# Block inverse of a chunked RWKV recurrence: products over four array quadrants, both head groups as one, identity preset by GpSimd, masked copies

## The chip, the cores and the metric

One core of a Trainium2 chip runs the whole program. Its engines are TensorE (PE in the profile, its weight loads PEld), VectorE (DVE), ScalarE (ACT), GpSimd (POOL) and SyncE (SP). The metric is device microseconds of one execution; lower is better. All tensors named here are float32, and each float32 product of 64x64 blocks leaves two matmul records and two weight-load records in the trace.

## The reference, cut to what matters

The reference is one mixer-and-feed-forward block followed by a two-layer block with experts. The change touches one piece alone: the two RWKV recurrences of the second block's first layer (forward and reversed), over 8 heads of 64 and 768 tokens (256 context tokens, then 512).

```python
def wkv7_scan(state0, r, w, k, v, a_vec, b_vec, reverse):
    def step(S, inp):
        r_t, w_t, k_t, v_t, a_t, b_t = inp
        sa = jnp.einsum('bhij,bhj->bhi', S, a_t)
        S = (S * w_t[:, :, None, :] + sa[..., None] * b_t[:, :, None, :]
             + v_t[..., None] * k_t[:, :, None, :])
        return S, jnp.einsum('bhij,bhj->bhi', S, r_t)
    s_fin, ys = lax.scan(step, state0, xs, reverse=reverse)
```

The kernel doesn't walk token by token. It takes chunks of 64 tokens, and inside a chunk the feedback of `sa` on itself is a unit lower triangular 64x64 system for each head and direction, which it inverts.

## The kernel before, in words

The program is a list of stages, and each stage writes out by hand what TensorE, ScalarE, VectorE and GpSimd do, in order, with semaphores between them. An engine's queue is strictly in the written order, so a wait holds up all that is written behind it. The recurrence is the stage `Wkv` (lines 1960 to 2325), and no other stage runs beside it. It makes `STEPS` = 768/64 = 12 steps, one for each chunk.

In a step there are 16 blocks of 64x64: tile `c` (4), head `e` in the tile (2), direction `d` (2). The 16 blocks of one kind lie in 128 partitions x 512 columns. A product whose operands are read from partitions 64i and whose result is written to partitions 64j uses the array's quadrant (row half i, column half j).

A step n, in the order of the work:
1. ScalarE `exps` (lines 2169, 2170), GpSimd `keyed` and `more_factors` (2290 to 2304), and VectorE `new_keys` and `factors` (2207 to 2226) make the decayed operands `at`, `rt`, `bt`, `kt`; for step n+1 they run inside step n.
2. TensorE multiplies operands against each other, "grams" (`gram`, line 2044). Kinds 0 and 1 give the triangular matrix L and its transpose; kinds 2 to 4 give matrices for values and outputs. Line 2059 transposes `vc`, `bt`, `kt` (12 transposes of 128x128), which ScalarE copies out of PSUM (2176).
3. VectorE masks gram 0 to `lt` and gram 1 to `x`, masks `lt` to `xt`, and adds the identity to both (2231, 2238, 2240, 2241). `x` is the inverse so far and `xt` its transpose.
4. Five levels (`LEVELS`) double the size of the inverted blocks. In each, GpSimd masks the blocks that join (2319, `lo`), TensorE multiplies `lo` by `x` (`half`), ScalarE copies the result to `t1` (2181), TensorE multiplies `t1` by `xt` and `xt` by `t1` (`whole`), and VectorE adds the results to `x` and `xt` (2250, 2251).
5. The right side (`from_state` 2104 and 2108, `from_keys` 2115 and 2120) is copied (2187) and multiplied by the inverse (the last use of line 2071, giving `u`), copied (2191), and goes into the state's and the output's sums (2140, 2145, 2150). VectorE adds and decays the state (2265, 2268) and adds the output to `y` (2273).

Steps 3 and 4 run for two groups `g`: tiles 0 and 1, then tiles 2 and 3, each 256 columns wide. The products of the inverse all go through one helper, which reads partitions of direction d and writes partitions of direction d, so it uses two quadrants:

```python
def diagonal(out, lhs, rhs, g, start=True, stop=True):
    for c in (2 * g, 2 * g + 1):
        for e in (0, 1):
            for d in (0, 1):
                last = t.matmul(self.by_token(out, c - 2 * g, e, d), self.by_token(lhs, c, e, d), ...
```

At a step's start TensorE waits for `factors`, multiplies grams 0 and 1 of group 0, waits for `y_added` of the step before (the output sums share PSUM banks 0 and 1 with group 1's grams), and goes on.

## Time and profile before

| what | us |
|---|---|
| median of 3 runs | 3028.18 (3023.76 to 3029.92) |
| the profiled execution | 3029.54 |
| its span, first to last instruction | 3027.8 |
| the stage `Wkv` in it, 1388.2 to 1754.7 | 366.5 |
| one step in it that kept the full clock, 1573.04 to 1602.76 | 29.72 |
| PE busy over the span, share | 2583.5, 85% |
| DVE / ACT / POOL busy, share | 1751.9, 58% / 1192.6, 39% / 388.3, 13% |

The profiled execution takes 1.7 us more than its span, and 1.4 us more than the median. Times in the trace count from the span's start. PE busy counts a matmul from its start to its modelled end; matmuls overlap, so the share of busy time is not the share of the peak. The granted clock (PEclk) is 1.00 at 2.4 GHz and 0.50 at 1.2 GHz.

### The profile page before, as it was taken

Reading aid. Unit: us, or ns where it says so; the run is one execution under the profiler, and the core shown is the slowest. Engines: PE = TensorE matmul, PEld = TensorE weight load, DVE = VectorE, ACT = ScalarE, POOL = GpSimd, SP = SyncE. Lnnn points to the kernel's source line nnn. Section 1 sums busy time; section 2 is a strip of 40 time slices with the busy share of each in tenths; the row PEclk is TensorE's granted clock in tenths of the full one; section 3 lists DMA queues with packets and bytes.
Section 4 is the critical chain, followed back from the end, with each engine's and each line's share of the span. In section 5 each row is a group of like instructions: output and inputs, shape, how many; then the busy total and the mean of one; then the engine's idle time right before and its main releaser. Section 6 shows DMA issues by size and latency. Waiting matters only on the chain.

```text
span 3027.8 us, 55155 instructions
## 1 busy us (share of the span) xinstructions
PE 2583.5 (85%) x23020; PEld 1975.1 (65%) x23020; DVE 1751.9 (58%) x2676; ACT 1192.6 (39%) x1719; POOL 388.3 (13%) x447
## 2 busy tenths in 40 slices
PE   6979779999976899988888887889976889978995
PEld 5745457777764457855777755767765656756774
DVE  3655554445433654446777664579975265447985
ACT  2423432223132155233222223267754247435773
POOL 1010010000011110003343401111111030011211
PEclk9978989999998799987999988999997989989998
DMA  4257722222210000100000031189992200017996
GB/s 167 90 182 283 288 70 84 83 83 111 83 58 32 6 1 38 34 22 2 4 4 4 4 140 47 63 350 400 403 368 96 77 1 2 29 61 289 407 389 235
DMA packets 63817, 385.10 MB, mean 127 GB/s; under 512 B 7840, under 2 KB 7856, under 8 KB 27104
## 3 DMA queue, kind: packets, MB, share of 16 engines
q1 hardware_dynamic: 41792, 292.60, 25.2%
q0 software_dynamic: 21792, 89.16, 7.7%
q8 instruction: 175, 2.87, 0.4%
q14 instruction: 58, 0.48, 0.0%
HBM read 344.99 MB, written 36.70 MB: 126 GB/s over the span
## 4 chain that ended last, share of the span: by engine, by line
PE 68%; DVE 10%; issue 4%; DVEq 4%; ACT 4%; PEld 3%; DMA 2%; POOL 1%; PEldq 1%; ACTq 1%; POOLq 0%; SPq 0%
PE psum L396 15%; PE psum L598 12%; PE psum L2985 6%; PE psum L2071 4%; PE psum L1124 4%; PE psum L3006 3%; PE psum L1143 2%; PE psum L1134 2%; PE psum L1763 2%; PE psum L2633 2%; PE psum L378 2%; PEld psum L2985 2%; PE psum L1670 2%; DVEq L2252 1%; PE psum L982 1%
## 5 line engine op out<-in xcount | busy, mean ns | idle before, releaser
L396 PE MATMUL psum<-arena_r 128*128 128x512 f32 (+1 forms) x976 | 311.4, 360 | 9.0 <-issue 4.0
L598 PE MATMUL psum<-arena_r 128*128 128x512 f32 x704 | 250.3, 396 | 27.4 <-DVE weight_slots_r L683 13.8
L396 PE MATMUL psum<-arena_r,weight_slots_r 128*128 128x512 f32 (+1 forms) x696 | 247.9, 356 | 0.0
L416 ACT ACTIVATE arena_r<-weight_slots 128x1024 fp32r<-128x1024 f32 x73 | 76.4, 1057 | 341.1 <-PE psum L396 255.6
L396 PEld LDWEIGHTS psum<-arena_r 128*128 128x128 f32 x976 | 178.9, 190 | 46.6 <-issue 20.2
L598 PE MATMUL psum<-arena_r,weight_slots_r 128*128 128x512 f32 x528 | 207.2, 392 | 0.0
L2071 PE MATMUL psum<-x_t 64*64 64x64 f32 x5376 | 180.3, 220 | 30.7 <-DVEq L2252 15.2
L2071 PEld LDWEIGHTS psum<-x_t 64*64 64x64 f32 x5376 | 166.4, 135 | 42.6 <-DVEq L2252 20.1
L396 PE MATMUL psum<-h_t_r,arena_r 128*128 128x512 f32 (+1 forms) x528 | 191.1, 362 | 0.3
L2957 DVE TENSOR_TENSOR weight_slots_r<-weight_slots,arena_r 128x2048 fp32r<-128x2048 f32 x78 | 177.5, 2287 | 17.8 <-ACT arena_r L2952 17.5
L2957 DVE TENSOR_TENSOR weight_slots_r<-weight_slots,h_t_r 128x2048 fp32r<-128x2048 f32 x72 | 164.1, 2288 | 19.8 <-ACT h_t_r L2952 19.2
L598 PEld LDWEIGHTS psum<-arena_r 128*128 128x128 f32 x704 | 132.3, 190 | 63.8 <-issue 31.9
L1208 DVE TENSOR_REDUCE stat<-psum 128x1 f32<-128x768 f32 (+1 forms) x112 | 98.7, 882 | 108.9 <-PE psum L1124 108.8
L2985 PE MATMUL psum<-weight_slots_r,arena_r 128*128 128x512 f32 x400 | 158.4, 396 | 0.0
L2952 ACT ACTIVATE arena_r<-weight_slots 128x2048 fp32r<-128x2048 f32 x78 | 148.6, 1912 | 24.2 <-DMA weight_slots<-in_weights 24.0
L2952 ACT ACTIVATE h_t_r<-weight_slots 128x2048 fp32r<-128x2048 f32 x72 | 137.2, 1913 | 26.3 <-DMA weight_slots<-in_weights 26.2
L396 PEld LDWEIGHTS psum<-arena_r,weight_slots_r 128*128 128x128 f32 x696 | 132.0, 190 | 18.9
L2985 PE MATMUL psum<-arena_r 128*128 128x512 f32 x416 | 135.1, 407 | 10.7 <-issue 10.2
L598 PE MATMUL psum<-h_t_r,arena_r 128*128 128x512 f32 x352 | 138.0, 392 | 0.0
L1124 PE MATMUL psum<-arena 64*128 64x384 f32 (+2 forms) x416 | 121.9, 535 | 8.6 <-POOL arena L1174 4.9
L2985 PE MATMUL psum<-h_t_r,arena_r 128*128 128x512 f32 x384 | 120.7, 395 | 2.1 <-issue 1.8
L421 DVE TENSOR_TENSOR weight_slots_r<-weight_slots,arena_r 128x1024 fp32r<-128x1024 f32 x73 | 88.4, 1220 | 53.1 <-ACT arena_r L416 52.2
(455 smaller groups left out, 5442.6 us busy)
## 6 DMA issues: line engine op xcount, KB each, us to landing
weight_slots<-in_weights SPq DMA_DIRECT2D x277, 1024.0 KB, 7.3
y_rows<-arena POOLq DMA_DIRECT2D x50, 512.0 KB
h_rows<-arena POOLq DMA_DIRECT2D x10, 512.0 KB, 3.0
x_keep<-x_t POOLq DMA_DIRECT2D x1, 3072.0 KB, 9.0
x_t<-x_keep POOLq DMA_DIRECT2D x1, 3072.0 KB, 14.5
x_t<-in_x POOLq DMA_DIRECT2D x1, 2048.0 KB, 10.0
out_x<-x_t SPq DMA_DIRECT2D x1, 2048.0 KB, 7.2
arena<-in_toe POOLq DMA_DIRECT2D x1, 1792.0 KB, 8.6
```

The costliest lines, as they stand in the source:

```text
L378: last = self.nc.tensor.matmul(self.bank(n), w[:, kt, :], self.operand(part, kt, a, b), start=(kt == order[0] and i == 0), stop=(kt == ord ...
L396: last = self.nc.tensor.matmul(self.bank(n), w[:, kt, :], self.operand(part, kt, a, b), start=(i == 0), stop=(i == len(passes) - 1))
L416: self.nc.scalar.activation(self.w_hi[:, t % 2], self.tile_weights(self.kern.slots, t), ACT.Copy).then_inc(self.rounded[0], 1)
L421: self.nc.vector.tensor_tensor(out=self.tile_weights(self.kern.slots_r, t), in0=self.tile_weights(self.kern.slots, t), in1=self.w_hi[:, t ...
L598: last = nc.tensor.matmul(bank, w(p, k), x(q, k), start=(k == j == 0), stop=(k == n - 1 and j == 2))
L1124: last = t_.matmul(s[:, r, a:b], q, key[:, a:b], start=True, stop=True)
L1208: v.reduce_max(kern.row_max[:, par], self.score_bank(u), mybir.AxisListType.XY)
L2071: last = t.matmul(self.by_token(out, c - 2 * g, e, d), self.by_token(lhs, c, e, d), self.by_token(rhs, c, e, d), start=start, stop=stop)
L2952: self.nc.scalar.activation(self.weights(item)[0], x, ACT.Copy).then_inc(self.rounded[0], 1)
L2957: self.nc.vector.tensor_tensor(out=self.kern.slots_r[:, slot, :], in0=self.kern.slots[:, slot, :], in1=hi.bitcast(F32), op=ALU.subtract).t ...
L2985: last = nc.tensor.matmul(ps[t % 2], x[:, t % 2, kt * P:(kt + 1) * P], w[:, k, :], start=(kt == 0 and i == 0), stop=(kt == KT - 1 and i == 2))
L3006: last = nc.tensor.matmul(ps[5 + half], x[:, t % 2, k * P:(k + 1) * P], w[:, k, half * 512:(half + 1) * 512], start=(k == 0 and i == 0), s ...
```

## The change

The stage `Wkv` alone is changed; its inputs and results are the same.

- **Four quadrants.** `plain` and `turned` are two layouts of the 16 blocks in 128x512. In `plain` (used for `lt`, `lo`, `x`) block (c, e, d) stands in the rows of d; in `turned` (used for `xt`, `t1`) in the rows of `home(c, d)`, which swaps the halves for odd c. `half`, `grow` and the product for `u` then read one half and write either, in an order that goes round the four quadrants. `grow_turned` reads and writes the same half.
- **Both head groups as one.** Each of `half`, `grow`, `grow_turned`, the copies, masks and additions is one instruction or batch for all 16 blocks, 512 columns wide. `grow` comes before `grow_turned`, each signals by itself, and the next `half` waits for the addition to `x` alone.
- **Preset and masked copies.** GpSimd writes the identity to `x` and `xt`; VectorE then copies the masked blocks of gram 1, and of a third gram for `xt` (`turned_gram`, 16 more products), over it with `copy_predicated`. The masks of `lt` to `xt` and the additions of the identity are gone.
- **Other products in the waits.** The products from the state and the keys stand in levels 1 to 4 between `half` and `grow`, where TensorE waits for ScalarE's copy. Grams 0 and 1 of step n+1 stand between the last level and `u` of step n; the masks of step n+1 stand before VectorE's state and output additions of step n.
- **Moved.** The key scaling goes from VectorE (`tensor_scalar`) to ScalarE (`scaled`); `y_added` is waited for before the transpose of `kt`; GpSimd's key totals come after its second level mask.

The core of the diff ("..." marks what is left out):

```diff
+    @staticmethod
+    def home(c, d):
+        return d ^ (c % 2)
+    def plain(self, x, c, e, d):
+        at = c // 2 * 256 + self.home(c, d) * P + e * 64
+        return x[64 * d:64 * d + 64, at:at + 64]
+    def turned(self, x, c, e, d):
+        r, at = 64 * self.home(c, d), c // 2 * 256 + d * P + e * 64
+        return x[r:r + 64, at:at + 64]
...
+        units = [(2 * a + (d ^ r), e, d) for a in (0, 1) for e in (0, 1) for d, r in corners]
...
+                for c, e, d in units:
+                    last = t.matmul(bank_of(6, d, c, e, self.home(c, d)), self.plain(w.lo[lv % 2], c, e, d), self.plain(w.x, c, e, d),
+                                    start=True, stop=True)
+                last.then_inc(self.sem("level_half"), 1)
...
+            def grow(lv):
+                for c, e, d in units:
+                    last = t.matmul(bank_of(4, self.home(c, d), c, e, d), self.turned(w.xt, c, e, d), self.turned(w.t1, c, e, d),
+                                    start=True, stop=True)
+                last.then_inc(self.sem("level_summed"), 1)
+            def grow_turned(lv):
...
+                    last = t.matmul(self.turned(psum[:, 3, :], c, e, d), self.turned(w.t1, c, e, d), self.turned(w.xt, c, e, d),
...
+            pe.wait_ge(*self.at("more_factors", n))
+            turn(6, w.vc)
+            turn(7, w.bt)
+            if n:
+                pe.wait_ge(*self.at("y_added", n - 1))
+            turn(0, w.kt)
+            pe.wait_ge(*self.at("masked", n, 2))
...
             for lv in range(self.LEVELS):
-                half(lv, 0)
-                half(lv, 1)
-                whole(lv, 0)
-                whole(lv, 1)
+                half(lv)
                 if lv == 0:
-                    gram(4, 0)
-                    gram(4, 1).then_inc(self.sem("last_grams"), 1)
-                if lv == self.LEVELS - 2:
-                    from_state()
-                    from_keys()
...
+                    gram(n, 4).then_inc(self.sem("last_grams"), 1)
+                if lv == 1:
+                    w_from_state()
+                if lv == 2:
+                    w_from_keys(0)
+                if lv == 3:
+                    w_from_keys(1)
+                if lv == last_lv:
+                    y_from_state()
+                ready(lv)
+                if lv < last_lv:
+                    grow(lv)
+                grow_turned(lv)
+            if n + 1 < self.STEPS:
+                first_grams(n + 1)
...
+            if n + 1 < self.STEPS:
+                turned_gram(n + 1).then_inc(self.sem("grams"), 1)
+                pe.wait_ge(*self.at("masked", n + 1, 1))
...
+            mask(0, w.lt, w.strict).then_inc(self.sem("masked"), 1)
+            dve.wait_ge(*self.at("presets", n, 0))
+            v.copy_predicated(out=self.four(w.x), mask=spread(w.first_low.bitcast(I32)),
+                              data=self.by_head(*self.GRAMS[1])).then_inc(self.sem("masked"), 1)
...
+            if more:
+                low(n + 1)
+                new_keys(n + 1)
+                up(n + 1)
+            state(n)
+            outputs(n)
...
+        def preset_plain(n):
+            if n:
+                pool.wait_ge(*self.at("level_half", n - 1, self.LEVELS - 1))
+            preset(w.x)
+        def preset_turned(n):
+            if n:
+                pool.wait_ge(*self.at("u_summed", n - 1))
+            preset(w.xt)
```

How the order moves. TensorE, from the last level of a step to the first of the next, before (2071 are the inverse's products, the pair of x32 and x16 the last level and `u`; 2140, 2145, 2150 the state and output; 2044 grams; 2059 transposes):

```order
L2071 MATMUL psum<-x_t 64x64 x32
L2071 MATMUL psum<-arena,x_t 64x64 x16
L2140 MATMUL psum<-arena 64x64 x16
L2145 MATMUL psum<-arena 64x64 x16
L2150 MATMUL psum<-arena 64x64 x16
L2044 MATMUL psum<-rstd,arena 64x64 x8
L2044 MATMUL psum<-arena,rstd 64x64 x8
L2044 MATMUL psum<-rstd,arena 64x64 x8
L2044 MATMUL psum<-arena,rstd 64x64 x8
L2059 MATMUL psum<-consts,arena 128x128 x12
L2044 MATMUL psum<-rstd,arena 64x64 x32
```

And now (2098 `half`, 2145 `y_from_state`, 2119 `grow_turned`, 2071 grams, 2203 `u`, 2080 `turned_gram`, 2211 to 2220 state and output, 2086 transposes):

```order
L2098 MATMUL psum<-x_t 64x64 x16
L2145 MATMUL psum<-rstd,arena 64x64 x16
L2119 MATMUL psum<-x_t 64x64 x16
L2071 MATMUL psum<-rstd,arena 64x64 x16
L2071 MATMUL psum<-arena,rstd 64x64 x16
L2203 MATMUL psum<-arena,x_t 64x64 x16
L2080 MATMUL psum<-rstd,arena 64x64 x16
L2211 MATMUL psum<-arena 64x64 x16
L2153 MATMUL psum<-arena 64x64 x16
L2216 MATMUL psum<-arena 64x64 x16
L2220 MATMUL psum<-arena 64x64 x16
L2086 MATMUL psum<-consts,arena 128x128 x12
```

Grams 0 and 1 of the next step have moved from behind the output products to ahead of `u`, and 16 products of `turned_gram` are new. VectorE over the same place, before (2251 the last additions to `xt`; 2265, 2268 state; 2273 output; then masks and identity of group 0):

```order
L2226 TENSOR_TENSOR arena<-arena 128x512
L2251 TENSOR_TENSOR x_t<-x_t,psum 128x256 x2
L2265 TENSOR_TENSOR arena<-arena,psum 128x512
L2268 TENSOR_TENSOR arena<-arena 128x512
L2273 TENSOR_TENSOR h_t<-h_t,psum 128x4x64 x2
L2231 TENSOR_TENSOR x_t<-psum,arena 128x256 x2
L2238 TENSOR_TENSOR x_t<-x_t,arena 128x256
L2240 TENSOR_TENSOR x_t<-x_t,arena 128x256
L2241 TENSOR_TENSOR x_t<-x_t,arena 128x256
```

And now (2352 the addition to `xt`, 2307 the mask of gram 0, 2314 and 2320 the masked copies, 2289 new keys, 2326 and 2329 state, 2336 output):

```order
L2303 TENSOR_TENSOR arena<-arena 128x512
L2352 TENSOR_TENSOR x_t<-x_t,psum 128x512
L2307 TENSOR_TENSOR x_t<-psum,arena 128x512
L2314 COPY_PREDICATED x_t<-arena,psum 128x512
L2289 TENSOR_TENSOR arena<-arena 128x4x64 x2
L2320 COPY_PREDICATED x_t<-arena,psum 128x512
L2326 TENSOR_TENSOR arena<-arena,psum 128x512
L2329 TENSOR_TENSOR arena<-arena 128x512
L2336 TENSOR_TENSOR h_t<-h_t,psum 128x4x64 x2
```

The next step's masks and new keys now stand ahead of this step's state and output additions. Within a level VectorE has one addition to `x` and one to `xt`, each 512 wide, in place of two of each at 256.

## Rows read from the trace of the kernel before

**Rows 1.** The page: costliest groups (busy us, mean ns | idle before, releasers), `diagonal`'s.

```profile
L2071 PE MATMUL psum<-x_t 64*64 64x64 f32 x5376 | 180.3, 220 | 30.7 <-DVEq L2252 15.2 <-DVEq L2242 13.4 <-ACTq L2177 1.9
```

**Rows 2.** Windows: the clean step, the whole stage, and clock windows.

```profile
core 0: us, PE busy (x) PEld busy (x) DVE busy (x) ACT busy (x) POOL busy (x), PEclk, DMA share, GB/s
1573.04:1602.76 29.72, 24.82 (x890) 23.00 (x886) 21.23 (x50) 7.77 (x19) 12.31 (x17) 1.00 0.02 4
1388.20:1754.70 366.50, 301.26 (x10512) 280.28 (x10512) 257.16 (x588) 94.60 (x229) 148.13 (x204) 0.97 0.02 4
1513.87:1517.28 3.41, 1.86 (x76) 1.54 (x69) 2.84 (x7) 0.00 (x0) 0.48 (x1) 1.00 0.02 5
1517.28:1520.69 3.41, 3.41 (x63) 3.08 (x64) 3.01 (x7) 1.33 (x3) 1.64 (x3) 0.50 0.00 0
1722.08:1725.49 3.41, 1.66 (x91) 1.46 (x82) 2.84 (x6) 0.00 (x0) 0.27 (x1) 1.00 0.02 5
1725.49:1728.90 3.41, 3.41 (x48) 3.08 (x50) 2.74 (x7) 0.91 (x2) 1.28 (x3) 0.50 0.02 7
```

**Rows 3.** Timeline of one level: start, us, engine, line, tiles, count, idle before.

```profile
1588.98 3.18 PE L2071 MATMUL psum<-x_t 64*64 64x64 f32 x96 [0.52 <-DVEq L2252]
...
1589.71 0.38 ACT L2181 ACTIVATE x_t<-psum 128x256 f32<-128x256 f32 x1 [0.82 <-PE psum L2071]
...
1591.86 0.41 DVE L2250 TENSOR_TENSOR x_t<-x_t,psum 128x256 f32<-128x256 f32 x1
1592.18 0.41 DVE L2251 TENSOR_TENSOR x_t<-x_t,psum 128x256 f32<-128x256 f32 x1
1592.21 0.38 ACT L2181 ACTIVATE x_t<-psum 128x256 f32<-128x256 f32 x1 [2.12 <-PE psum L2071]
1592.68 2.41 PEld L2071 LDWEIGHTS psum<-x_t 64*64 64x64 f32 x80 [0.66 <-DVEq L2252]
```

**Rows 4.** Timeline: batches over two quadrants (2108) and over four (2044).

```profile
1595.53 1.10 PE L2108 MATMUL psum<-rstd,arena 64*64 64x64 f32 x32
...
1607.91 1.16 PE L2044 MATMUL psum<-rstd,arena 64*64 64x64 f32 x64 [0.35 <-DVEq L2242]
```

**Rows 5.** Groups by line and form inside the stage.

```profile
L2176 ACT ACTIVATE arena<-psum 128x512 f32<-128x512 f32 x33 | 17.3, 599 | 62.1 <-PE psum L2059 62.1
L2265 DVE TENSOR_TENSOR arena<-arena,psum 128x512 f32<-128x512 f32 x11 | 7.6, 688 | 20.3 <-PE psum L2145 20.3
L2300 POOL TENSOR_TENSOR arena<-arena 128x512 f32<-128x512 f32 x11 | 14.0, 1275 | 54.0 <-issue 54.0
L2293 POOL COPY arena<-arena 128x256 f32<-128x256 f32 x22 | 8.1, 400 | 1.8 <-issue 1.8
```

**Rows 6.** Timeline from the state's addition to the next step's first level.

```profile
1602.76 0.69 DVE L2265 TENSOR_TENSOR arena<-arena,psum 128x512 f32<-128x512 f32 x1 [1.79 <-PE psum L2145]
...
1603.53 0.69 DVE L2268 TENSOR_TENSOR arena<-arena 128x512 f32<-128x512 f32 x1
1604.34 0.93 DVE L2273 TENSOR_TENSOR h_t<-h_t,psum 128x256 f32<-128x256 f32 x2
1605.40 0.33 PEld L2044 LDWEIGHTS psum<-rstd,arena 64*64 64x64 f32 x16 [1.92 <-DVEq L2275]
...
1606.03 1.53 PE L2059 MATMUL psum<-consts,arena 128*128 128x128 f32 x12
...
1607.41 0.42 DVE L2241 TENSOR_TENSOR x_t<-x_t,arena 128x256 f32<-128x256 f32 x1
...
1608.48 2.46 POOL L2319 TENSOR_TENSOR x_t<-x_t,arena 128x256 f32<-128x256 f32 x3 [1.78 <-DVEq L2236]
...
1609.25 0.68 PE L2071 MATMUL psum<-x_t 64*64 64x64 f32 x16 [0.18 <-ACTq L2177]
...
1610.28 0.94 DVE L2241 TENSOR_TENSOR x_t<-x_t,arena 128x256 f32<-128x256 f32 x1
```

**Rows 7.** Timeline: transposes and grams where the clock is 0.50.

```profile
1516.86 2.47 PE L2059 MATMUL psum<-consts,arena 128*128 128x128 f32 x12
...
1519.26 1.79 PE L2044 MATMUL psum<-rstd,arena 64*64 64x64 f32 x64
```

**Rows 8.** Timeline: the first operation of the stage, and its first level on TensorE.

```profile
1388.24 2.13 DVE L2207 TENSOR_SCALAR arena<-weight_slots,arena 128x128 f32<-128x128 f32 x4 [0.79 <-ACTq L129]
...
1402.00 3.19 PE L2071 MATMUL psum<-x_t 64*64 64x64 f32 x94 [0.17 <-ACTq L2177]
```

400 lines of the change are left out of this document (217 added, 183 removed).

## The prediction

> **What bounds the kernel now.** I read the page's groups first. The one helper of the block inverse, line 2071, is the largest group in the stage `Wkv`: 5376 records, 180.3 us busy, and the engine idle for only 30.7 us before them [rows 1]. Then the windows: the stage takes 366.5 us, DMA is busy for 2% of it, so only the four engines matter, and a step at full clock takes 29.72 us, with PE busy 24.82 and DVE 21.23 [rows 2]. Then the timeline of one level [rows 3]. The same point of two levels in a row is 1588.98 and 1592.68, so a level takes 3.70 us. TensorE runs 96 records without a break in 3.18 of it and then waits 0.52 for VectorE. Both head groups are used to cover each other's copies, and the cover is so good that TensorE's own issue rate is the bound in a level. Outside the levels it isn't: from the state's addition (1602.76) to the next first level (1609.25) there are 6.49 us in which TensorE mostly waits for VectorE [rows 6].
>
> **The rate of a batch.** The 32 records over two quadrants take 1.10 us, 64 records over four take 1.16 [rows 4]. A single matmul takes 0.22 us [rows 1], so 32 records issue in 0.88 to 0.94 by the one and 64 in 0.94 by the other. I take for 16 products (32 records): 0.47 us of issue over four quadrants, 0.94 over two, and 0.22 from the last issue to the end. That is the gain the change is after. A level now issues 6 batches of 8 products over two quadrants, 6 x 0.47 = 2.82 us; after, `half` and `grow` cost 0.47 each, and `grow_turned` still uses two quadrants, 0.94, in all 1.88.
>
> **A level after.** With one group nothing covers the copies any more, so the chain counts, not the issue: `half` 0.47 + 0.22, ScalarE's start 0.10 later (taken from 1589.71, 0.73 after the batch's first record, in [rows 3]) and its copy 0.60 for 512 columns [rows 5], 0.05 to TensorE, `grow` 0.69, 0.05 to VectorE, its addition 0.69 for 512 columns [rows 5], 0.05 back. The sum is 2.92 us against 3.70. Under it lie: `grow_turned` (0.94 of issue behind `grow`, over before the addition to `x` ends), the addition to `xt` and the mask of a gram or the decayed operands on VectorE (0.69 each beside 2.92), the exponentials and scalings on ScalarE, the 512-wide level mask on GpSimd (1.28 for such an operation [rows 5], asked for two levels ahead), and the state and key products, which fit between `half` and the copy's end. One doesn't fit: `w_from_state` in level 1 waits for level 0's last mask, behind two additions on VectorE, and pushes `grow` by about 0.5. Four levels from `half` 0 to `half` 4: 4 x 2.92 + 0.5 + 0.1 = 12.3.
>
> The trace bears on a rule here. The copies out of PSUM are 0.60 + 0.69 of a level's 2.92 [rows 5]. The Trainium skill, TensorEngine Tiling (Array Packing), section Performance Considerations, says that tiling speeds up TensorE but not the evacuation of PSUM, which may become the bottleneck. Its table of speedups taken alone (twice for the second dimension, here on two of three batches) would be worth the whole 0.94 of issue in each of five levels, 4.7 us a step; its warning is what the chain shows, 0.78 a level.
>
> **The rest of a step after.** (a) Last level to `u`: `half` issue 0.47, then `y_from_state`, which goes from one half to the same half, 0.94; that about equals the wait for the copy (0.69 + 0.10 + 0.60 + 0.05 = 1.44). Then `grow_turned` 1.16, 0.05, the addition 0.69, 0.05: 3.3 us. (b) Grams 0 and 1 of the next step issue meanwhile (0.94) and end 0.2 after `u` starts. VectorE masks gram 0 (0.60 to its next operation) and copies masked to `x` (0.69); only then may TensorE write the state sums over their banks, at about 1.5 after `u`'s start. Three batches, 0.47 + 0.47 + 0.69, and 0.05: the state's addition starts 3.2 after `u`. (c) State and output additions: before, 2.64 from 1602.76 to TensorE at 1605.40 [rows 6]. Now GpSimd's first level mask of the next step runs beside the state's decay. A VectorE operation on two SBUF operands took 0.42 us at 1607.41 with GpSimd idle and 0.94 at 1610.28 beside it [rows 6]. I add 0.53 for the 512-wide one: 3.2. (d) `y_added` releases the last 4 transposes (a third of 1.53 [rows 6] less overlap, 0.43) and 64 records of grams, 0.94: 1.4 to `half` 0.
>
> Sum: 12.3 + 3.3 + 3.2 + 3.2 + 1.4 = 23.4 us a step, against 29.72: 6.3 less.
>
> The masks and additions of the identity (six operations a group, between `grams` and the first level) leave the path, because they are replaced by three 512-wide operations done under the previous step's end; the preset copies on GpSimd (twice 0.40 each for 512 columns, [rows 5]) end before VectorE needs them. The key scaling on ScalarE costs nothing: ScalarE is busy 7.77 of 29.72 us [rows 2]. `turned_gram` (0.47 of issue) lies in the wait for the masked copy. The added wait there holds up the key products, `y_from_keys` and the state products, and is in (b).
>
> **The unknown prices.** No row shows a masked copy. From below, 0.41, what the 256-wide addition takes [rows 3] (I see no reason for less); the nearest row is the 512-wide operation from PSUM, 0.69, and I take that. From above, twice it, 1.3, if it also reads what it overwrites. At 1.3 a step is 24.3, over twelve steps 10 us more; at 0.41 it is about 0.2 less a step, 2 us. The contention in (c) costs between 0 and 1.2, so -0.6 to +0.7 a step, -7 to +8 us.
>
> By the Trainium skill, SBUF — State Buffer, section Who interferes with whom, a VectorE instruction with two SBUF inputs contends with a GpSimd instruction that reads SBUF, and one with at most one SBUF input doesn't. By that rule the masked copy (mask in SBUF, data in PSUM) is free of GpSimd's preset beside it; no row here shows that.
>
> **The clock.** In the whole stage it is 0.97 [rows 2]. It fell twice in mid-stage, each time where the engine waited most: PE busy 1.86 and 1.66 of 3.41 us, from the outputs over the first grams to the transposes, and then 0.50 for 3.41 us [rows 2]. After the change the stretch from the output products to `half` 0 is of the same kind (transposes, a wait of about 1.2 us, four transposes), with the batches before it shorter. The two falls and the cold start are in the 366.5 already. A fall after the change would lie on (d): 0.43 of transposes and 0.94 of grams, all on the path, so about 1.4 more at half the clock. I allow for two more of them than now, 3 us.
>
> **The stage.** 11 step distances at 6.3 less make 69. The last step ends without a next: 25.6 us from its first level to the end before (23.2 to the state's addition, as 1609.25 stands 6.49 behind 1602.76 in a 29.72 step, and 2.5), after 12.3 + 3.3 + 3.2 + 3.1 = 21.9 less the 1.0 that the wait for the next step's masks took, so 4.7 less. The head, 13.8 us to the first level [rows 8], stays: the same operations in another order. 69 + 4.7 - 3 = 71. All else in the kernel is untouched and waits for the stage's end. The profiled execution took 3029.54, so 2958.5; it lies 1.4 above the median, which gives **2957 us**.
>
> **The rivals.**
> - *Forecast* (62%): 2957, its own range 2946 to 2970.
> - *VectorE's queue sets the end of the step* (20%): masked copies at the upper price, and contention with GpSimd twice what I put. Both masked copies, the new keys, state and outputs stand in one row there. For it speaks that VectorE is busy 21.23 of 29.72 already [rows 2]; against it, that the 512-wide forms save start-up. 26 us a step: saving 12 x 3.7 - 3 = 41, so 2987; halfway, 2972.
> - *The batches don't overlap as the grams do* (6%), the change not doing what it says: `half`, `grow`, `u` and `turned_gram` at the rate of two quadrants. Eleven batches of 0.47 more, about 5.2 us a step, 28.6: saving 12 x 1.1 = 13, 3015. Against it: the gram at line 2044 has the same pattern, row half to its own bank, all quadrants in turn [rows 4].
> - *Cheaper than thought* (7%): no contention in (c), masks hidden: 22.7, 2948 or a little less.
> - *The clock* (5%), the side of slower: with one group TensorE waits more than now, and if it stays at 0.50, each batch is dearer. 12 transposes took 2.47 in part at half clock against 1.53 [rows 6, 7], 64 records 1.79 against 1.16 [rows 4, 7], the latter in part cold too. Some 11.5 us of the chain are TensorE's; fully cold they'd be about 21.5 and a step 33.4. That is 3.7 over now, 12 x 3.7 = 44, so 3072. It decides where more than 6.3/10 = 63% of the stage is cold. Against it: in a level TensorE still issues for 1.9 to 2.3 of 2.9 us.
>
> **How the numbers follow.** Forecast and the cheaper case lie below 2970, and the second case spreads over 2966 to 2990. 2943 to 2980 leaves out about 2 in 10: the upper half of the second case, the third, the clock. A change within 0.2% (6 us) is about what a measurement can't tell from none. Faster: forecast, cheaper, second and nearly all of the third, 92%; same 4%; slower 4%.
>
> **What would show it.** Steps of 23.4 us from one state addition to the next (27 or more would break the forecast); levels of 2.9, with 32 records in 0.69; the masked copy at 0.69; the state's decay near 1.2 beside GpSimd; the granted clock 0.95 or more. If levels take 3.4 or more, the quadrants don't overlap; if the levels are right and the step isn't, it is VectorE's queue between the last addition to `xt` and `y_added`.

## The result, and the profile after

The changed kernel took 2994.90 us (median of four runs, 2991.75 to 3001.35), the kernel before 3027.57 (four runs). The ratio is 0.9892 [0.9871, 0.9912]: faster by 33 us, where 71 were forecast, and outside the range, which ended at 2980. The profiled execution of after took 2991.75 us.

The two stretches of eleven steps, from the first state addition to the last, in the windows view of the kernel before and then of after (columns: window, its length, then busy time and records of PE, PEld, DVE, ACT, POOL, then the granted clock, DMA share, GB/s):

```profile
1423.96:1752.09 328.13, 274.06 (x9648) 254.82 (x9640) 228.99 (x529) 84.40 (x207) 130.83 (x180) 0.99 0.02 4
```

```profile
1423.25:1718.05 294.80, 230.58 (x9907) 209.96 (x9901) 171.92 (x277) 89.25 (x170) 136.53 (x146) 0.99 0.02 5
```

A step went from 29.83 to 26.80 us; the forecast was 23.4. PE is busy 44 us less and DVE 57 us less, so the change removed the work that it should. The clock is the same. PE's records rose from 19288 to 19808, 1753 to 1801 a step. That is the number that I had not used.

The prices held. Groups of after by line and form, in the same stretch (columns as in [rows 1]):

```profile
L2260 ACT ACTIVATE x_t<-psum 128x512 f32<-128x512 f32 x55 | 32.8, 597 | 105.6 <-PE psum L2098 105.6
L2349 DVE TENSOR_TENSOR x_t<-x_t,psum 128x512 f32<-128x512 f32 x44 | 30.2, 686 | 40.2 <-PE psum L2111 40.1
L2314 DVE COPY_PREDICATED x_t<-arena,psum 128x512 f32<-128x512 int32 x10 | 7.2, 719 | 0.0
L2320 DVE COPY_PREDICATED x_t<-arena,psum 128x512 f32<-128x512 int32 x10 | 7.4, 740 | 3.2 <-POOL x_t L2396 1.3 <-issue 1.1 <-PE psum L2080 0.8
L2216 PE MATMUL psum<-arena 64*64 64x64 f32 x352 | 8.1, 220 | 4.7 <-issue 4.7
L2326 DVE TENSOR_TENSOR arena<-arena,psum 128x512 f32<-128x512 f32 x12 | 8.3, 689 | 16.8 <-PE psum L2216 16.8
```

The copy is 0.60 and the addition 0.69, as forecast. The masked copy, whose price no row of before showed, is 0.72 to 0.74. The row of L2216 shows what the forecast has no term for: ahead of the state's last products TensorE is idle for 4.7 us, and nothing that the profile knows ends it ("issue"). The state addition, the last row, waits for them.

Where this sits in a step, in PE's timeline of after (start, duration, line, count, idle before and what ended it). L2098 is `half`, L2111 `grow`, L2119 `grow_turned`:

```profile
1510.45 0.65 PE L2098 MATMUL psum<-x_t 64*64 64x64 f32 x32
...
1511.81 0.62 PE L2111 MATMUL psum<-x_t 64*64 64x64 f32 x25 [0.25 <-ACT x_t L2260]
1513.27 0.28 PE L2111 MATMUL psum<-x_t 64*64 64x64 f32 x4 [0.84 <-issue]
...
1514.41 0.69 PE L2098 MATMUL psum<-x_t 64*64 64x64 f32 x32
...
1517.95 0.69 PE L2098 MATMUL psum<-x_t 64*64 64x64 f32 x32
...
1526.78 0.52 PE L2071 MATMUL psum<-rstd,arena 64*64 64x64 f32 x19
1527.96 0.39 PE L2071 MATMUL psum<-rstd,arena 64*64 64x64 f32 x10 [0.67 <-issue]
...
1530.37 0.56 PE L2211 MATMUL psum<-arena 64*64 64x64 f32 x21 [0.56 <-DVE x_t L2314]
1531.44 0.39 PE L2211 MATMUL psum<-arena 64*64 64x64 f32 x10 [0.51 <-issue]
```

32 records run in 0.65 to 0.69 us, so the quadrants do overlap. But a batch of `grow` breaks off after 25 records, a gram 15 us later after 19, then the key products after 21. In the middle of a batch there is nothing to wait for. There are 46 such breaks in the eleven steps (more than 0.25 us from one record's start to the next's). The number of PE's records (matmuls and weight loads) from one to the next is always 253 to 256 or a multiple of that: 510 to the break at 1513.27, 508 to 1520.51 and to 1527.96, 256 to 1531.44. Where it is a multiple, the block's end in between fell where it shows no break. In the same stretch the queue of kind "instruction" moves packets of 0.016 MB, 64 bytes for each of 256 instructions (queue view of before's eleven steps, then of after's):

```profile
q8 instruction: 76, 1.25, 1.6%
```

```profile
q8 instruction: 78, 1.28, 1.9%
```

One packet in 4.32 us before, one in 3.78 us after. The Trainium skill, Advanced Engine Details and Errata, section ISA Cache, gives 16 KB or 256 instructions as the line in which an engine's instructions come, and two lines as all there are. The packets, and the distance of the breaks, agree with the first; experiment 2 bears on the second. **The theory** (instruction supply, "theory A" in the expectations): a block of 256 instructions takes a smallest time to come, called its turn here, and TensorE, which got quicker, has come up against it. The chain of work over this window (1511 to 1534) puts 11.7% on "issue". **The rival** (waits, "theory B"): the chain of the forecast was right in kind, but contention, VectorE's queue and the waits are longer than I priced them.

By the forecast's own cuts, the mean of ten steps of after, from the first records of the batches:

| stretch | forecast | after | of it gaps inside batches |
|---|---|---|---|
| `half` 0 to `half` 4 | 12.3 | 13.60 | 1.32 |
| `half` 4 to `u` | 3.3 | 4.27 | 0.66 |
| `u` to state addition | 3.2 | 4.64 | 1.48 |
| state addition to next `half` 0 | 4.6 | 4.74 | 0.34 |
| step | 23.4 | 27.25 | 3.80 |

(A gap is more than 0.25 us from the start of one record to the start of the next in one batch; transposes are not counted. The ten steps run from one `u` to the next and leave out the last, short one, hence 27.25 beside 26.80.) The miss is 3.85 us, the gaps are 3.80, and most of them lie where the miss is. That the two sums agree so closely is luck: the shortest of each stretch in after, 12.5 us for the four levels (2.87, 3.48, 3.25 and 2.91), 3.62, 3.68 and 4.21, add up to 24.0, so about 0.6 of the miss is chain that was priced too low, and at most 3.2 is what the gaps cost.

Where two breaks are one block apart (26 times), the second comes 3.44 to 4.02 us after the first, 3.72 in the mean. At that turn 1801 records take 26.2 us, nearly the whole step.

### The profile page after: what moved, and what is told of

It reads as the page before. It is cut to its first block, busy times and chain, and to the rows that moved or that the text cites. A ratio compares the mean times of both kernels' runs of the same rounds, so it can differ in the third digit from the quotient of the medians.

```text
span 2989.9 us, 55348 instructions
## 1 busy us (share of the span) xinstructions
PE 2538.2 (85%) x23404; PEld 1928.2 (64%) x23404; DVE 1687.0 (56%) x2400; ACT 1199.7 (40%) x1683; POOL 394.0 (13%) x411
## 3 DMA queue, kind: packets, MB, share of 16 engines
q1 hardware_dynamic: 41792, 292.60, 25.8%
q8 instruction: 178, 2.92, 0.4%
## 4 chain that ended last, share of the span: by engine, by line
PE 64%; DVE 9%; PEld 7%; issue 6%; ACT 5%; DMA 3%; DVEq 2%; PEldq 1%; POOL 1%; ACTq 1%; POOLq 0%; SPq 0%
PE psum L396 15%; PE psum L598 12%; PEld psum L3103 4%; PE psum L1124 4%; PE psum L3103 3%; PE psum L1143 3%; PE psum L1134 2%; PE psum L1763 2%; PE psum L2751 2%; PEld psum L3124 2%; PE psum L2119 2%; PE psum L378 2%; PE psum L1670 2%; DMA weight_slots<-in_weights 1%; PE psum L3124 1%
## 5 line engine op out<-in xcount | busy, mean ns | idle before, releaser
L3075 DVE TENSOR_TENSOR weight_slots_r<-weight_slots,h_t_r 128x2048 fp32r<-128x2048 f32 x72 | 163.4, 2286 | 13.9 <-ACT h_t_r L3070 13.7
L396 PEld LDWEIGHTS psum<-arena_r,weight_slots_r 128*128 128x128 f32 x696 | 132.1, 190 | 18.9
L598 PEld LDWEIGHTS psum<-arena_r,weight_slots_r 128*128 128x128 f32 x528 | 99.9, 189 | 21.2
L698 DVE TENSOR_TENSOR arena<-arena,psum 128x512 f32<-128x512 f32 x22 | 15.1, 688 | 174.1 <-ACT arena L663 174.1
```

The lines of the kernel that those rows point to most:

```text
L396: last = self.nc.tensor.matmul(self.bank(n), w[:, kt, :], self.operand(part, kt, a, b), start=(i == 0), stop=(i == len(passes) - 1))
L598: last = nc.tensor.matmul(bank, w(p, k), x(q, k), start=(k == j == 0), stop=(k == n - 1 and j == 2))
L3075: self.nc.vector.tensor_tensor(out=self.kern.slots_r[:, slot, :], in0=self.kern.slots[:, slot, :], in1=hi.bitcast(F32), op=ALU.subtract).t ...
```

## The experiments

All are told by the step, taken between state additions of the profiled execution, beside the ratio of the runs to those of before. The totals carry noise from elsewhere: two executions of one kernel (`a_best`, `best_again` below) stood so ahead of the stage, in the windows of 1200 to 1388 us (the last three columns are clock, DMA share, GB/s):

```profile
1200.00:1388.00 188.00, 165.64 (x892) 127.19 (x896) 87.06 (x116) 59.82 (x95) 12.23 (x13) 0.91 0.10 37
```

```profile
1200.00:1388.00 188.00, 169.91 (x807) 127.25 (x808) 81.20 (x106) 52.05 (x81) 7.35 (x6) 0.87 0.10 37
```

Just ahead of the stage the clock was at 0.50 for 17 us in the one and for 44 in the other, and the first state addition stood at 1411.31 and at 1426.24. Inside the stage stretches of 3.41 us at 0.50 of the clock (cold stretches) fall here and there; I give their number. Two profiled executions of after itself lie 1 us a step apart (experiment 8), so a difference of less than that between two single profiles is not shown by them.

**1. A stream of products, by itself (`m1_stream`).** The heart of the kernel, for four quadrants:

```
corners = ((0, 0), (1, 1), (0, 1), (1, 0))
...
            for i in range(n):
                r, q = corners[i % 4]
                at = i // 4 % 4 * 64
                last = t.matmul(ps[64 * q:64 * q + 64, r, at:at + 64], a[64 * r:64 * r + 64, at:at + 64],
                                b[64 * r:64 * r + 64, at:at + 64], start=True, stop=True)
```

> This kernel computes no part of the reference: after eight 512-column products it issues, with nothing to wait for, 768 products of 64x64x64 (fp32, four matmuls each in the records) that alternate over four array quadrants, then 768 over two quadrants, then 512 of 128 moving columns over four quadrants, then 384 of 64 columns over four quadrants again. Theory A (instruction supply: TensorE's instructions arrive in packets of 16384 bytes on the queue of kind instruction, 256 of them every 3.45 to 3.7 us, and the engine outruns them): four quadrants at 64 columns go in turns of about 3.5 us for 256 instructions (32 products at 8 instructions each), the records filling 1.6 to 2.2 us and a gap of 1.3 to 1.9 us closing the turn; 768 products take about 42 us for 12 groups of 64 if a product is four instructions, about 84 us if it is eight. Two quadrants come to about 3.75 us for each 64 products by their records, so hardly any gap. Theory B (the gaps belong to the waits and the contention of the recurrence's own code): no gaps without a wait; four quadrants at 0.55 to 0.60 us for 16 products, so 26 to 29 us for the 768; two quadrants 1.10 for 16 or 53 us.

Groups of its page (L29 four quadrants, L37 two, L45 four with 128 moving columns), then the timeline of the first stream, then windows over the first three streams, then the queue in the first window:

```profile
L29 PE MATMUL ps_h<-b_h,a_h 64*64 64x64 f32 x2304 | 37.9, 219 | 23.5 <-issue 23.5
L37 PE MATMUL ps_h<-b_h,a_h 64*64 64x64 f32 x1536 | 45.2, 218 | 0.2 <-issue 0.2
L45 PE MATMUL ps_h<-b_h,a_h 64*64 64x128 f32 x1024 | 28.2, 269 | 0.0
```

```profile
11.38 3.25 PE L29 MATMUL ps_h<-b_h,a_h 64*64 64x64 f32 x207
...
15.75 2.09 PE L29 MATMUL ps_h<-b_h,a_h 64*64 64x64 f32 x128 [1.12 <-issue]
...
19.20 2.09 PE L29 MATMUL ps_h<-b_h,a_h 64*64 64x64 f32 x128 [1.36 <-issue]
...
22.66 2.09 PE L29 MATMUL ps_h<-b_h,a_h 64*64 64x64 f32 x128 [1.36 <-issue]
...
26.11 2.09 PE L29 MATMUL ps_h<-b_h,a_h 64*64 64x64 f32 x128 [1.36 <-issue]
...
50.84 0.93 PE L29 MATMUL ps_h<-b_h,a_h 64*64 64x64 f32 x49 [1.36 <-issue]
```

```profile
11.38:51.54 40.16, 24.87 (x1534) 23.39 (x1537) 0.00 (x0) 0.00 (x0) 1.00 0.02 4
51.54:96.71 45.17, 44.96 (x1551) 44.83 (x1545) 0.00 (x0) 0.00 (x0) 1.00 0.02 5
96.71:124.66 27.95, 27.95 (x1034) 27.95 (x1033) 0.00 (x0) 0.00 (x0) 1.00 0.02 5
```

```profile
q8 instruction: 11, 0.18, 1.8%
```

With nothing to wait for, 128 matmuls and 128 weight loads run in 2.09 us, and the next 128 start 3.45 us after the first. The stream starts with 415 records that have no break; from 15.75 to 50.84 it makes ten turns of exactly 256 records, 3.51 us each in the mean (3.45 to 3.73). The 768 products took 40.2 us, near theory A's 42 and not the 26 to 29 of theory B. Two quadrants take 45.2 us with one gap, at their start, or 3.73 a block: on a stream of products this small four quadrants are worth 11%, and 6% once the turns have set in, not a factor of two. So the supply's limit is shown without the recurrence. Of the two counts that I left open, four instructions a product is right. The 128-column stream goes at 3.49 us for 64 products without a gap, twice the columns in the time in which the 64-column one waits.

**2. How far ahead (`m2_bursts`).** The same products in bursts with pauses.

> This kernel computes no part of the reference: TensorE issues bursts of products of 64x64x64 over four quadrants (four instructions each), six bursts of 128 products with pauses of about 7 us between them, then eight of 64 products with pauses of about 3.5 us. Form 1 of the supply theory (one block of 256 instructions ahead of the one that runs, the next is fetched only once a block is entered): after a pause 256 to 512 instructions go at full speed, 1.87 us for 256, so each burst of 512 has one gap of 1.3 to 1.6 us, at the second block's end that it reaches, and takes about 5.2 us; the pause does not buy a third block; a burst of 256 after a pause of 3.5 us has no gap or one of up to 0.4 us. Form 2 (a steady rate with a deeper store, filled in pauses): the bursts of 512 instructions run through in 3.7 us, without a gap.

PE's timeline:

```profile
10.29 3.25 PE L33 MATMUL ps_h<-b_h,a_h 64*64 64x64 f32 x207
14.74 0.93 PE L33 MATMUL ps_h<-b_h,a_h 64*64 64x64 f32 x49 [1.20 <-issue]
24.75 5.84 PE L33 MATMUL ps_h<-b_h,a_h 64*64 64x64 f32 x256 [9.07 <-DVE o_h L63]
39.67 6.65 PE L33 MATMUL ps_h<-b_h,a_h 64*64 64x64 f32 x256 [9.07 <-DVE o_h L63]
```

Its queue from 24.7 to 39.6 us, a burst of 512 instructions and its pause:

```profile
q8 instruction: 2, 0.03, 0.8%
```

The first burst has its one gap, 1.20 us, after 415 records, and the fifth (70.24) one of 0.43 at the same place. In the others the clock fell (0.54 and 0.67 in the windows of the second and third), and 512 instructions took 5.8 to 6.7 us, or about as long for 256 as they need to come, so the durations tell nothing: that half is inconclusive, and so are the bursts of 256. The packets tell more: the second burst's two packets start at 27.28, once it has run 2.5 us, and at 30.77, and the rest of a 9 us pause brings none; the next comes at 42.22, inside the third burst. A pause buys nothing beyond the block in hand and the next.

**3. Sixteen products more, in a wait (`a_pad`).**

```diff
+            pe.wait_ge(*self.at("masked", n, 2))
+            gram(n, 2)
             if n:
                 pe.wait_ge(*self.at("y_added", n - 1))
```

> The changed kernel with 16 products more in each of the twelve steps: the products of the gram of keys and decayed removals are issued twice, once more ahead of the wait for the outputs of the step before, into the same banks; 64 more TensorE instructions a step, in a wait that is 0.8 to 1 us long. Its output is the reference's. Theory A (instruction supply: a step lasts as long as its instructions take to arrive, about 3.5 us for 256): 64/256 of 3.5, or 0.9 us a step, 10 to 11 us in all, though the wait covers the products. Theory B (the step is a chain of waits, and what is issued into a wait costs nothing): 0 to 2 us in all.

2996.98 us, 0.9896 [0.9879, 0.9912]; 26.86 us a step, no cold stretch. The theory's 0.9 us was wrong, the rival's 0 right. The theory as I had written it (a step lasts as long as its instructions take) is too simple: 1865 records a step at the stream's 3.51 us for 256 are 25.6 us, still under the step, and the place is one where TensorE idles for VectorE anyway. With one block ahead, time is lost only where 256 instructions would run in less than a turn. I took this second form from here on. What was expected of experiments 4 and 5 had been worked out by the first form, so that they came near it is in part luck.

**4. Sixteen products fewer (`a_less16`),** the line `y_from_state()` taken out.

> The changed kernel without one batch of 16 products a step, the state's part of the outputs, which stands in the wait for the last level's half (so y lacks r times the state; the output is not the reference's). No other engine has more or less to do. Theory A (instruction supply): 64 instructions fewer a step, 0.9 us a step, 10 to 11 us less. Theory B (chain of waits): the batch lies beside ScalarE's 0.60 us copy and takes 0.55 to 0.70 us, so at most 0.1 us a step, 0 to 1.2 us in all.

2990.57 us, 0.9886 [0.9868, 0.9904]; 25.98 us a step, 0.82 less than after, with two cold stretches against after's one. The theory said 0.9, the rival at most 0.1. `half` 4 to `u` went from 4.27 to 3.51 us, and its gaps from 0.66 to 0.09; the shortest such stretch fell too, from 3.62 to 3.36, so about 0.3 of it is the batch's own time on the chain, where the rival had 0.1 at most. The medians don't show the gain: 0.9886 beside 0.9892 is 2 us, with intervals 5 us and more to either side.

**5. The same work in fewer instructions (`a_merged`).** The grams `kt` with `at` and `kt` with `rt` have one stationary operand (`both` holds `at` and `rt`):

```diff
+        def key_grams(n):
+            both = w.both[:, :, n % 2, :]
...
+                    last = t.matmul(out, self.by_dim(w.kt, c, d, e), both[64 * e:64 * e + 64, :, c * P + d * 64:c * P + d * 64 + 64],
+                                    start=True, stop=True)
...
-            gram(n, 2)
-            gram(n, 3).then_inc(self.sem("more_grams"), 1)
+            key_grams(n).then_inc(self.sem("more_grams"), 1)
```

> The changed kernel with two grams that share their stationary operand, keys with removals and keys with readings, as one batch of 16 products of 128 moving columns instead of 32 of 64 columns; the gram of additions with readings takes the later place, in the wait for the first level's half, and GpSimd's next product waits for it there. Same arithmetic, 64 TensorE instructions a step fewer, the same columns. Theory A (instruction supply): 0.9 us a step, 10 to 11 us less than the changed kernel, about 2985 us. Theory B (chain of waits): ahead of the first level now stand 16 products of 128 columns where 32 of 64 stood, the same 1.1 to 1.2 us: 0 within 2 us, and up to 0.2 us a step slower if the two operands' strided columns cost time.

2988.18 us, 0.9869 [0.9852, 0.9886]; 25.67 us a step with two cold stretches, 1.13 less than after, with nothing left out (in the medians 7 us, and the intervals overlap):

```profile
1423.43:1705.75 282.32, 227.16 (x9553) 209.16 (x9548) 174.55 (x276) 89.07 (x170) 138.88 (x147) 0.99 0.02 5
```

PE is busy only 3.4 us less than in after over the eleven steps, but they are 12.5 us shorter. Gaps inside batches fell from 3.80 to 2.56 us a step.

**6. Two quadrants at a time (`a_twoq`).**

```diff
-        units = [(2 * a + (d ^ r), e, d) for a in (0, 1) for e in (0, 1) for d, r in corners]
+        units = [(2 * a + (d ^ r), e, d) for pair in (corners[0:2], corners[2:4]) for a in (0, 1) for e in (0, 1) for d, r in pair]
```

> The changed kernel with its level batches in another order: the same 16 products, but alternating over two array quadrants (eight products), then over the other two, where they went round all four. Same instructions, results and waits. By the rows of the two orders a batch goes from 0.65 to 0.70 us to about 1.10 us. Theory B (the chain decides): the half 0.41 us later and the growing batch 0.41 us later, some 0.8 us for each of four levels, 0.4 for the last, 0.4 for u: 4 us a step, 30.8 us, about 48 us slower than the changed kernel. Theory A (a level waits for its instructions, 3.45 us for 256): the batches' longer time falls first into the time that was lost anyway; a level comes to 3.75 to 3.9 us where it is 3.45 to 3.6, so 1 to 1.6 us a step, 28 us, 12 to 20 us slower.

3002.20 us, 0.9898 [0.9871, 0.9924]; 27.37 us a step. The rival's 30.8 is far off; the theory's 28 was still too much. Gaps fell from 3.80 to 2.05 us a step, the levels took 14.38 for 13.60. The heading of the change, four quadrants where there were two, is worth about 0.6 us a step by this profile in place of the 4 by the rates; with two executions of after 1 us apart, and ratios of 0.9898 beside 0.9892 and 0.9900, it can't be told from nothing.

**7. The chain shortened (`a_early`), and both together (`a_best`).**

```diff
-                pe.wait_ge(*self.at("y_added", n - 1))
-            turn(0, w.kt)
+                pe.wait_ge(*self.at("state_added", n - 1))
...
+            turn(4, w.kt)
...
+                    if n:
+                        pe.wait_ge(*self.at("y_added", n - 1))
                     gram(n, 4).then_inc(self.sem("last_grams"), 1)
...
-            y_from_keys()
             pe.wait_ge(*self.at("u_copied", n))
...
             last.then_inc(self.sem("state_summed"), 1)
+            y_from_keys()
```

> The changed kernel with the step's end in another order, same results and same instructions: the 16 products of values and masked key gram that go into the outputs stand behind the state's last products rather than ahead of them, and the keys' transposes go to a bank that the state addition frees (a semaphore of its own after that addition), where they waited for both additions to the outputs. On the chain by the rows of after: 0.5 to 0.9 us earlier state addition, and transposes and grams 1 to 2.5 us earlier. Theory B (the chain decides): 1.5 to 2.5 us a step, 24.3 to 25.3 us. Theory A (instruction supply: 1816 instructions a step at 3.45 us for 256 are 24.5 us, and what is pulled together outruns it more often): it gives 0.5 to 1.3 us, and no step mean under 24.5 us; 25.5 to 26.3 us.

> The same new order of the step's end on top of the kernel with the merged key grams (1752 instructions a step, 23.6 us of supply). Theory A: not under 23.6 us a step; 24.2 to 24.8 us where the merged kernel had 25.7, so 10 to 17 us less than it: 2971 to 2978 us. Theory B: the order gives its full 1.5 to 2.5 us a step here as in the kernel without the merge, 23.2 to 24.2 us, 2962 to 2971 us. In either theory the lowest time so far.

`a_early`: 2993.40 us, 0.987 [0.9844, 0.9896]; 26.89 us a step, no gain at all, below what either theory gave. `u` to state addition went from 4.64 to 3.84, state addition to `half` 0 from 4.74 to 4.56, and both came back: the levels rose from 13.60 to 14.40, and the gaps from 3.80 to 5.51. A chain was shortened by about 1 us and the instructions took it: 53 breaks now stand one block apart, where after has 26, in eleven steps of some 77 blocks.

`a_best`: 2980.58 us, 0.9833 [0.9809, 0.9857], the fastest kernel up to here that leaves nothing out; 25.40 us a step without a cold stretch, where the theory wanted 24.2 to 24.8 and the rival 23.2 to 24.2. Both were wrong: the nine steps of `a_merged` without a cold stretch took 25.26, so the profiles show no gain from the new order here either. The medians lie 8 us apart, with intervals that overlap. Its profiled execution is 2964.41, of which 15 us are the clock ahead of the stage.

**8. Again, beside each other (`after_again`, `best_again`), and one more batch moved (`a_best2`).**

> The changed kernel once more, to stand on the same chip and in the same rounds beside the next two: 2992 to 2998 us, its steps 26.6 to 27.0 us in the mean, and gaps of TensorE inside batches of 3.5 to 4 us a step.

> The kernel with the merged key grams and the new order of the step's end once more, on the same chip as the changed kernel. Its steps were 25.4 us where the changed kernel's were 26.8, 1.4 x 12 = 17 us less: 2976 to 2981 us beside 2992 to 2998.

> As the kernel before it in this call, and the turned gram of the next step (16 products, and VectorE's copy of it) behind the state's last products rather than between u and them. On the chain 16 products and up to 0.74 us of VectorE less between u and the state addition: about 1.3 us a step. The waits' theory: 24.1 us a step, 15 us less in all than the kernel before it. The supply theory: its 1752 instructions a step need 24.5 us at the 3.58 us for 256 of the stream, the gaps inside batches grow by most of what the chain loses: 24.9 to 25.3 us a step, 1 to 6 us less in all.

After again: 3005.66 us (2981.06 to 3006.12), 0.9900 [0.9867, 0.9933], 27.80 us a step with six cold stretches; five steps free of them took 27.86 in the mean, and why they are 1.1 us above those of the first execution is open. `best_again`: 2981.77 us, 0.9835 [0.9808, 0.9861], 25.67 a step with one cold stretch. The two intervals don't touch: 2 us a step and 24 us in the medians. After came out slower than expected, and that is part of the 24. `a_best2`: 2979.86 us, 0.9838 [0.9810, 0.9866], 26.08 a step. `u` to state addition fell again, from 3.67 to 3.25, and the step didn't. The waits' theory wanted 24.1, the supply theory 24.9 to 25.3: neither was right. In steps without a cold stretch it took 25.9, `best_again` 25.5.

**9. Inside the levels (`a_less32`, `a_less16_b`, `a_less32_b`, `a_nofill`).** `a_less32` also leaves out both `w_from_keys`, `a_nofill` `w_from_state` too.

> The kernel without the state's part of the outputs (as in the run that left it out alone), and now also without the two half batches of 8 products a step that add the values to the removals' sum (so the values' part of it is missing, and the output is not the reference's). They stood in the waits for the second and third level's half, beside ScalarE's copy of 0.60 us, at 0.25 to 0.30 us of TensorE each. Theory A in its second form (256 instructions take 3.45 us to arrive, one block ahead, so time is lost only where 256 would otherwise run in less; the levels are such a place): 64 instructions fewer inside the levels, up to 0.86 us a step less than the 26.0 us of the run without the outputs' part, 25.1 to 25.5 us. Theory B (waits and contention make the steps long): the two half batches are hidden by the copy; 26.0 us a step within 0.1.

> The kernel without the state's part of the outputs once more (its output is not the reference's), because its profile and that of the kernel with two more half batches left out held two and five stretches of 3.41 us at half the granted clock, so that 26.0 and 26.2 us a step can't be set against each other. Expected in the steps without such a stretch: 25.5 us, as there.

> The kernel without the state's part of the outputs and without the values' part of the removals' sum (output not the reference's), once more for the same reason. Supply theory: 0.4 to 0.8 us a step below the kernel above it in this call, in steps without a cold stretch: 24.7 to 25.1 us. Waits' theory: as the one above, 25.5 us within 0.2.

> The kernel without the state's part of the outputs, and without any part of the removals' sum: neither values nor state go into it (what ScalarE copies in its place is what the bank held; the output is not the reference's). Between the second level and the last nothing but the levels' own 48 products, 192 instructions, is left to TensorE: at 3.45 us for 256 they need 2.6 us, less than the 2.92 us of the prediction's chain. Supply theory: the four levels from the first half to the last go from 13.1 to 13.6 us to 12.0 to 12.5 us (the first level keeps its 64 products), with 0 to 0.4 us of gaps inside their batches; a step 24.3 to 25.0 us. Waits' theory: what was left out stood beside ScalarE's copy; the four levels stay at 13.1 us or more, the step at 25.5 us.

| kernel | median, ratio | step (cold stretches) | steps without | `half` 0 to 4 | gaps |
|---|---|---|---|---|---|
| `a_less16` | 2990.57, 0.9886 [0.9868, 0.9904] | 25.98 (2) | 25.5 | 13.14 | 2.64 |
| `a_less16_b` | 2986.67, 0.9856 [0.9840, 0.9873] | 25.93 (4) | 25.3 | 13.28 | 2.47 |
| `a_less32` | 2977.63, 0.9828 [0.9797, 0.9860] | 26.16 (5) | 25.5 | 13.36 | 2.07 |
| `a_less32_b` | 2971.64, 0.9815 [0.9762, 0.9869] | 25.73 (3) | 25.8 | 13.26 | 1.89 |
| `a_nofill` | 2971.61, 0.9815 [0.9796, 0.9835] | 24.83 (3) | 24.4 | 12.58 | 1.66 |

Between the first and the second pair the supply theory missed: 64 instructions fewer in the second and third level took 0.6 us of gaps away, and the step didn't follow. (The medians do differ, by 13 and 15 us, but the profiled steps don't show it, and the runs of `a_less32_b` spread over 31 us.) The last kernel came out nearly where the supply theory said: 24.83 us a step, the levels at 12.58 (it wanted 12.5 at most) with 0.58 of gaps (it wanted 0.4 at most). But this doesn't decide between the theories, because something else went too: `w_from_state` waits for a mask of VectorE, the 0.5 us of the forecast's sum. In after:

```profile
1515.93 0.69 PE L2137 MATMUL psum<-arena,rstd 64*64 64x64 f32 x32 [0.82 <-DVE arena L2307]
```

L2137 is `w_from_state`, in the second level. With it that level never took less than 3.47 us in any execution but that of `a_early` (3.42); in `a_nofill` it took 2.92 at best, and 3.11 in the mean where `a_less32` had 3.64. That is most of the 0.7 to 0.8 us by which the levels got shorter, and the rival explains it as well. The last level of `a_nofill`:

```profile
1507.91 0.69 PE L2098 MATMUL psum<-x_t 64*64 64x64 f32 x32 [0.23 <-DVE x_t L2340]
1509.33 0.69 PE L2111 MATMUL psum<-x_t 64*64 64x64 f32 x32 [0.72 <-ACT x_t L2252]
1509.84 1.10 PE L2119 MATMUL psum<-x_t 64*64 64x64 f32 x32
1510.83 0.69 PE L2098 MATMUL psum<-x_t 64*64 64x64 f32 x32
```

1507.91 to 1510.83 is 2.92 us, the forecast's level to the hundredth. After reaches it too: its shortest fourth level is 2.91 and its shortest first level, with 256 instructions, 2.87. The chain of a level was priced right, and it holds wherever no block ends inside it.

All profiles together show the supply best. By instructions a step and steps without a cold stretch: 1816 and more, 26.8 to 27.9 us (after twice, `a_pad`, `a_twoq`, `a_early`); 1752, 25.3 to 25.9 us (`a_less16` twice, `a_merged`, `a_best` twice, `a_best2`), with the chain in three different orders; 1688, 25.5 and 25.8; 1624, 24.4. The first two groups don't touch.

## Why the prediction was wrong, point by point

- **The prices** were right: `half` and `grow` 0.65 to 0.69 for 32 records, copy 0.60, addition 0.69, masked copy 0.72 to 0.74 (taken 0.69). The level of 2.92 is what the first and the fourth level take when no block ends inside. Two terms of the sum were low: the third level never took less than 3.25 in after, and `u` to state addition never less than 3.68, where 3.2 was forecast.
- **State addition to `half` 0**, (c) and (d): 4.6 forecast, 4.74 measured; 6.49 before [rows 6]. Of the 3 us that a step gained, 1.75 come from here, where identity and masks left the path. Within it the term for contention was about right in the mean: the state's decay, 0.69 in every step before, took 0.69 to 1.73 in after (1.05 in the mean of the eleven steps), that is +0.36 where I had +0.53.
- **The step that failed** is "With one group nothing covers the copies any more, so the chain counts, not the issue". From `half` 0 to the state addition it gave 18.8 us; before took about 23.2, after 22.5. The issue does count, but by another limit than the array's: 256 instructions come in 3.45 us at best, 3.51 in the mean of the stream and 3.72 in after where breaks are one block apart. The first two levels hold 256 of them each in 2.92 and 3.42 us of chain, the next two 224 each in 2.92, and the stretch from the next step's first grams to the outputs some 500, for which the forecast had about 5 us. I had priced each batch by how fast its records follow each other in one batch of 64 records [rows 4], and summed to times that a long run of records can't keep. That cost at most 3.2 of the 3.85 us a step.
- **Was it to be seen before?** In part. The 1.16 us batch of [rows 4] is 128 instructions, too short to show the limit. So are 256, of which before runs some 270 records in 1.90 us in one place:

```profile
1631.17:1633.07 1.90, 1.90 (x135) 1.90 (x134) 0.59 (x1) 0.64 (x2) 0.00 (x0) 1.00 0.05 9
```

  But in the eleven steps of before no 512 records run in under 5.7 us, and no 1024 in under 13.9, 3.5 for 256. And a step of 1753 records and one packet in 4.32 us stood in the trace, and its batches over two quadrants, 0.94 us of issue for 32 records and as many weight loads, need 3.8 us for 256, so the kernel before ran just slower than its supply. A forecast of 23.4 us for 1801 records asks for 3.33 us for 256 as a mean over the whole step, waits included, less than the 3.45 that the stream gets at best. With the stream's mean of 3.51 that division alone gives a floor of 24.7 us a step, 12 x 1.3 = 16 us above my forecast, 2973, still inside the range. The rest, 2.1 us a step in the profiled execution, is in part the longer turn in the kernel, and in part that the supply is only one block ahead of a step that is part waits and part bursts; the runs don't divide it.
- **VectorE's queue** had 20% for this outcome in size (26 us a step) but was not the cause: before the state addition VectorE waits for TensorE (16.8 us over the twelve), and masked copies cost the middle price. My last sentence, that levels of 3.4 or more would mean that the quadrants don't overlap, was a wrong test: levels are 3.2 to 3.65 in the mean, 13.60 for four, and the quadrants overlap.
- **The clock**: 0.99 in the eleven steps, one cold stretch, as allowed for.
- **Open** stays why leaving out 8 + 8 products in levels 2 and 3 gave nothing a step, why two executions of after differ by 1 us in steps of full clock, and the last 0.5 to 1 us between the runs with fewer instructions and the chain. All three have to do with a turn that isn't one number: between breaks one block apart it is 3.72 us in after and 3.83 in its second execution, 3.74 and 3.71 in the two of `a_less16`, 3.83 and 3.82 in the two of `a_less32`. What sets it no run shows.

## What to carry to other kernels

Before a chain of small products is summed up, count the instructions of the engine in it (a 64x64x64 product in fp32 is four on TensorE) and divide by what its instruction queue has been seen to deliver; if the sum runs faster than that, the sum is not the time. Where that is the bound, sharing a stationary operand between two products pays though it saves no column, a batch hidden in a wait can be free (`a_pad`) or not (`a_less16`), and a shorter chain may give nothing back (`a_early`, and `a_best` beside `a_merged`). And when a batch is left out to test a theory, look whether a wait went with it (`a_nofill`).

## What the runs showed of the hardware

- TensorE's instructions come in packets of 256, one in 3.45 us where nothing else holds it (15.75 to 19.20), 3.51 in the mean of ten. Small fp32 products over four quadrants run 256 in 2.09 us and then wait. The Trainium skill, Runtime: NRT & Kernel Launch, section Instruction fetch mechanics, says that the fetch is hidden because the sequencer dispatches slower than it fills; in this stream the trace disagrees, 23.5 us of idle time in 61.
- The fetch isn't done far ahead: a 9 us pause brought no third packet (`m2_bursts`).
- Products of 64 columns over two quadrants (3.73 us for 64) fall just outside the limit, and so do those of 128 columns over four (3.49).
- A masked copy of 128x512 from PSUM takes 0.72 to 0.74 us, also beside GpSimd's preset. A multiplication of two SBUF operands of that size took 0.69 to 1.73 us with GpSimd's level masks beside it.
